# Turning activation blocks by DMA instead of by TensorE: B/C rows, three residual blocks ahead of each MLP, the fourth ahead of the gates

## What is computed

```python
def mamba2_mixer(hn, w_in, conv_w, ...):
    zxbcdt = hn @ w_in
    xbc = jax.nn.silu(causal_depthwise_conv(xbc, conv_w, conv_b))   # xs, bm, cm are parts of xbc
    ...
def sq_relu_mlp(hn, w1, w2):
    return jnp.square(jax.nn.relu(hn @ w1)) @ w2
def per_layer_input(h, p_i, g, w_gate, w_proj):
    gate = jax.nn.sigmoid(rmsnorm(h, g) @ w_gate)
    return h + gate * (p_i @ w_proj)
def reference(...):
    for i in range(DEPTH):
        h = h + mixer(rmsnorm(h, ln_mix[i]))
        h = h + sq_relu_mlp(rmsnorm(h, ln_mlp[i]), mlp_w1[i], mlp_w2[i])
        h = per_layer_input(h, p[i], ple_norm[i], ple_gate_w[i], ple_proj_w[i])
    return h
```

## Time and profile before

| | us |
|---|---|
| median of 3 runs | 2545.94 (2545.83 to 2546.37) |
| the profiled execution | 2546.43 |
| its span, first to last instruction | 2544.7 |
| PE busy | 2537.2 |
| DVE busy | 1646.3 |
| ACT busy | 1339.2 |
| mean busy share of the DMA queue of SP | 68.7% |

### The profile page before, as it was taken

One profiled execution on the slowest core, in us unless ns is written; L12 is line 12 of the kernel. 1 busy time (PEld: TensorE's weight loads), 2 busy tenths in 40 slices (PEclk: granted clock), 3 DMA queues, 4 the chain that ended last, 5 costly groups with the idle time before them and its releaser, 6 DMA issues.

```text
span 2544.7 us, 29493 instructions
## 1 busy us (share of the span) xinstructions
PE 2537.2 (100%) x11668; PEld 2113.4 (83%) x11668; DVE 1646.3 (65%) x1735; ACT 1339.2 (53%) x1674; POOL 100.5 (4%) x208
## 2 busy tenths in 40 slices
PE   9999999999999999999999999999999999999999
PEld 8888888888888888888888888888888888888887
DVE  7678878888755565565557667766655655546564
ACT  6555556656544454443546657655544434434553
POOL 2010000000000000000000002100000000000000
PEclk9999999999999999999999999999999999999999
DMA  8688887887586776776777764446867767767763
GB/s 262 198 246 242 240 244 236 235 231 212 175 229 200 198 217 199 200 219 195 209 213 213 209 188 141 140 154 191 220 192 203 217 193 211 209 194 219 211 207 133
DMA packets 350250, 524.49 MB, mean 206 GB/s; under 512 B 108432, under 2 KB 113800, under 8 KB 350112
## 3 DMA queue, kind: packets, MB, share of 16 engines
q1 hardware_dynamic: 345936, 512.39, 68.7%
q0 software_dynamic: 2656, 8.58, 1.3%
q10 hardware_dynamic: 1520, 1.64, 0.2%
HBM read 486.38 MB, written 2.16 MB: 192 GB/s over the span
## 4 chain that ended last, share of the span: by engine, by line
PE 100%; DMA 0%; DVE 0%; ACT 0%; ACTq 0%; issue 0%
PE acc_a L1936 13%; PE acc_a L1938 13%; PE acc_a L1937 13%; PE acc_b L1936 13%; PE acc_b L1938 13%; PE acc_b L1937 13%; PE mid L1938 5%; PE mid L1936 5%; PE mid L1937 5%; PE tp L1983 1%; PE mid L2116 1%; PE acc_b L2055 1%; PE mid L2319 0%; PE tp L2339 0%; PE tp L2113 0%; DMA h<-in_x 0%
## 5 line engine op out<-in xcount | busy, mean ns | idle before, releaser
L1270 DVE TENSOR_TENSOR w<-raw,w 128x1024 fp32r<-128x1024 f32 (+1 forms) x872 | 1058.6, 1220 | 770.4 <-ACT w L679 767.7
L679 ACT ACTIVATE w<-raw 128x1024 fp32r<-128x1024 f32 (+1 forms) x872 | 916.0, 1055 | 996.2 <-PE acc_b L1938 411.4
L1936 PE MATMUL acc_a<-w,xa 128*128 128x512 f32 x768 | 301.8, 393 | 0.0
L1938 PE MATMUL acc_a<-w,xa 128*128 128x512 f32 x768 | 299.2, 390 | 0.0
L1937 PE MATMUL acc_a<-w,xa 128*128 128x512 f32 x768 | 298.9, 389 | 0.0
L1936 PE MATMUL acc_b<-w,ya_hi 128*128 128x512 f32 x736 | 288.4, 392 | 0.0
L1938 PE MATMUL acc_b<-w,ya_lo 128*128 128x512 f32 x736 | 286.6, 389 | 0.0
L1937 PE MATMUL acc_b<-w,ya_hi 128*128 128x512 f32 x736 | 286.4, 389 | 0.0
L1936 PE MATMUL acc_b<-w,xa 128*128 128x512 f32 (+1 forms) x728 | 282.8, 388 | 0.0
L1938 PE MATMUL acc_b<-w,xa 128*128 128x512 f32 (+1 forms) x728 | 280.1, 385 | 0.0
L1937 PE MATMUL acc_b<-w,xa 128*128 128x512 f32 (+1 forms) x728 | 279.8, 384 | 0.0
(11 more groups left out here) (332 smaller groups left out, 2934.9 us busy)
## 6 DMA issues: line engine op xcount, KB each, us to landing
raw<-in_mlp_w SPq DMA_DIRECT2D x512, 512.0 KB, 4.0
raw<-in_ssm_in_w SPq DMA_DIRECT2D x161, 512.0 KB, 5.7
raw<-in_ssm_out_w SPq DMA_DIRECT2D x64, 512.0 KB, 5.7
raw<-in_ple_gate_w SPq DMA_DIRECT2D x64, 512.0 KB, 4.2
raw<-in_mla_out_w SPq DMA_DIRECT2D x32, 512.0 KB, 3.7
rows<-in_ssm_conv_w SPq DMA_DIRECT2D x32, 256.0 KB, 6.5
scratch<-cumulative POOLq DMA_DIRECT2D x16, 512.0 KB, 7.1
raw<-in_ple_proj_w SPq DMA_DIRECT2D x8, 512.0 KB, 4.4
```

What stands on the lines that cost most here:

```text
L679: act.activation(w_hi[:, g % SPL, :, 0:cols], raw[:, g % RAW, :, 0:cols], ACT.Copy)\
L1270: dve.tensor_tensor(w_lo[:, g % SPL, :, 0:cols], raw[:, g % RAW, :, 0:cols], w_hi[:, g % SPL, :, 0:cols].bitcast(F32), ALU.subtract).then_ ...
L1936: pe.matmul(dst, xh, wh, start=first and k == 0, stop=False)
L1938: mm = pe.matmul(dst, xl, wh, start=False, stop=last and k == 1)
```

## The change

What it does, by places:

- The B and C rows are turned by DMA: `row_words_out` on ACT (2 copies for each block), 2 transposing DMAs on SP, `join_rows` on DVE, in buffers of their own, and the convolution reads `row_joined`. `turn_rows` goes from PE. The convolution's taps stand behind three rests instead of one.
- Of the four blocks ahead of each MLP, block 0 is still turned by PE; blocks 1 to 3 by DMA. The first two up units are interleaved (`UP_FIRST`): 4 chunks read block 0, 4 read block 1, and so on.
- Block 3 ahead of the gates is turned by DMA; the first two gate units are interleaved by `DOWN_FIRST`, so that block 3 is first read in chunk 12.
- `words` and `turned` become two buffers each. Words of block n still wait for the join of block n-2 (`jn`).
- POOL issues its first decay transfer ahead of its wait for the convolved B and C.

In all PE loses 12 turns of 8 transposes, and ACT, SP and DVE get 12 turned blocks more (53 instead of 41).

```diff
+UP_FIRST = [(j, k) for blk in range(4) for j in range(2) for k in (2 * blk, 2 * blk + 1)]
+UP_TURNS = (8, 10, 12), (6, 8, 11)
...
@@ SP
+            def turn_rows():
+                sp.wait_ge(S["rwd"], w.tick("rwd") + 1)
+                for t in range(NT):
+                    sp.dma_start_transpose(row_turned[...], row_words[:, t]...).then_inc(S["rtr"], 16)
...
-                unit(up, c512(0))
+                for m, (j, k) in enumerate(UP_FIRST):
+                    load(u[:, 2 * k:2 * k + 2, c512(512 * j)])
+                    if m in UP_TURNS[layer]:
+                        turn_block()
...
+                for m, (n, k) in enumerate(DOWN_FIRST):
+                    load(g[:, 2 * k:2 * k + 2, c512(512 * n)])
+                    if m in (1, 9):
+                        turn_block()
@@ POOL
-            pool.wait_ge(S["si"], 4)
+                if i == 0:
+                    pool.wait_ge(S["si"], 4)
@@ ACT
                 def job(before=None):
+                    n = w.tick("wd")
+                    words = words_of_two[n % 2]
                     act.wait_ge(S["hadd"], w.now("hadd") + 1)
-                    act.wait_ge(S["jn"], w.tick("wd"))
+                    if n > 1:
+                        act.wait_ge(S["jn"], n - 1)
...
-                unit({2: [act_hi(tiles(xa, 2))], 3: [product(0)]}, halves=4)
-                jobs = {m: [own_before(product(m + 1), 4)] for m in range(3)}
-                jobs[3] = [sums(n, 3), act_hi(tiles(xa, 3))]
+                unit({0: [own_before(product(1), 4)], 1: [own_before(product(2), 4), words_of(3), sums(n, 3)],
+                      2: [own_before(product(3), 4)], 6: [act_hi(tiles(xa, 3))]}, halves=16)
...
-            mlp(0, "BA", {1: [sums(1, 1), act_hi(tiles(xa, 1))], 3: [sums(1, 2), act_hi(tiles(xa, 2))],
-                          5: [sums(1, 3), act_hi(tiles(xa, 3))]})
+            mlp(0, "BA", {0: [words_of(1), sums(1, 1)], 2: [words_of(2), sums(1, 2)], 4: [words_of(3), sums(1, 3)],
+                          5: [act_hi(tiles(xa, 1))], 8: [act_hi(tiles(xa, 2))], 10: [act_hi(tiles(xa, 3))]})
...
-            unit({4: [sums(4, 0), act_hi(tiles(xa, 0))], 6: [sums(4, 1), act_hi(tiles(xa, 1))]}, halves=7)
-            mlp(1, "AB", {1: [sums(4, 2), act_hi(tiles(xa, 2))], 4: [sums(4, 3), act_hi(tiles(xa, 3))]})
+            unit({4: [sums(4, 0), act_hi(tiles(xa, 0))], 5: [words_of(1), sums(4, 1)]}, halves=7)
+            mlp(1, "AB", {0: [words_of(2), sums(4, 2)], 3: [act_hi(tiles(xa, 1)), words_of(3), sums(4, 3)],
+                          5: [act_hi(tiles(xa, 2))], 8: [act_hi(tiles(xa, 3))]})
@@ DVE
-            mlp(0, "BA", {0: [lo(tiles(xa, 0))], 1: [add_out(2), gain(V_MLP + 4), add_out(3)], 2: [lo(tiles(xa, 1))],
-                          3: [gain(V_MLP + 8)], 4: [lo(tiles(xa, 2))],
-                          5: [gain(V_MLP + 12)], 6: [lo(tiles(xa, 3))]})
+            mlp(0, "BA", {0: [lo(tiles(xa, 0))], 1: [add_out(2)], 3: [add_out(3)], 4: [join, in_gain(4)],
+                          6: [lo(tiles(xa, 1))], 7: [join, in_gain(8)], 8: [lo(tiles(xa, 2))],
+                          9: [join, in_gain(12)], 11: [lo(tiles(xa, 3))]})
...
+            mlp(1, "AB", {1: [lambda before: add("B", 3, 0)(before)], 2: [join, in_gain(20)], 3: [lo(tiles(xa, 1))],
+                          4: [join, in_gain(24)], 6: [lo(tiles(xa, 2))], 7: [join, in_gain(28)], 9: [lo(tiles(xa, 3))]})
@@ PE
-            out_piece(OUT_TAIL[2], {3: [turn_h(0, 29)], 6: [turn_h(1, 30)]})
+            out_piece(OUT_TAIL[2], {3: [turn_h(0, 29)]})
...
-                up(0, turns, needs(posted))
+                for j, k in UP_FIRST:
+                    if j == 0 and k % 2 == 0:
+                        pe.wait_ge(S["act"], need[k // 2])
+                    chunk(xa, 2 * k, pairs[j], k == 0, k == 7)
...
-                    if n == 1:
-                        turn_h(3, base + 4)()
-                unit(xa, pp[0], "gs", None, [c + 1, c + 3, c + 4, c + 5])
+                for n, k in DOWN_FIRST:
+                    if n == 0 and k % 2 == 0:
+                        pe.wait_ge(S["act"], need[k // 2])
+                    chunk(xa, 2 * k, pp[n], k == 0, k == 7)
...
-                if n:
-                    turn_h(n - 1, 60 + n)()
+                if n == 1:
+                    turn_h(0, 61)()
```

More of the change, by code:

```diff
@@ L190, in trunk_kernel @@
         at[0] = 0
-        prj, p_sb = part(NT, D), part(NT, PLE)
-        words = part(NT * 512).bitcast(U16).rearrange("p (t s n) -> p t s n", t=NT, s=2)
-        turned = part(4 * TOK).bitcast(U16).rearrange("p (s f n) -> p s f n", s=2, f=4)
+        prj = part(NT, D)
+        p_sb = r_sb[:, 0, :].rearrange("p (t n) -> p t n", t=NT)
+        words_of_two = [part(NT * 512).bitcast(U16).rearrange("p (t s n) -> p t s n", t=NT, s=2) for _ in range(2)]
+        turned_of_two = [part(4 * TOK).bitcast(U16).rearrange("p (s f n) -> p s f n", s=2, f=4) for _ in range(2)]
         joined = part(4, TOK)
@@ L209, in trunk_kernel @@
         ksq = sqf[:, :, 0:512]
-        table = [part(NT, HALF) for _ in range(4)]
+        table = [hq[:, n].rearrange("p (t d) -> p t d", t=NT) for n in range(4)]
         acc_a, acc_b = [ctx.enter_context(nc.psum_tensor(f"acc_{n}", [P, 2, 512], F32)) for n in "ab"]
@@ L253, in trunk_kernel @@
             "wd",
-            "tr",
             "jn",
@@ L280, in trunk_kernel @@
             "xr",
-            "Tc",
+            "rwd",
+            "rtr",
+            "rjn",
             "c0",
@@ L333, in trunk_kernel @@
             "To")}
+        s_turned = [sem(f"turned{n}") for n in range(2)]
         s_lag = [None] + [sem(f"lagged{n}") for n in range(1, CONV_W)]
@@ L480, in gates @@
                     load(v[:, :, c512(512 * n)])
-                for n in range(NB):
-                    jobs = {1: [turn_block]} if n == 0 else {5: [turn_block]} if n > 1 and layer == 0 else {}
-                    unit(ple_gate_w[layer], c512(512 * n), 0, jobs)
+                g = row_tiles(ple_gate_w[layer])
+                for m, (n, k) in enumerate(DOWN_FIRST):
+                    load(g[:, 2 * k:2 * k + 2, c512(512 * n)])
+                    if m in (1, 9):
+                        turn_block()
+                unit(ple_gate_w[layer], c512(2 * 512))
+                unit(ple_gate_w[layer], c512(3 * 512), 0, {3: [turn_block], 6: [turn_block]} if layer == 0 else None)
             mlp(0)
@@ L2173, in mlp @@
                 base = 32 + 32 * layer + 12
-                up(0, turns, needs(posted))
+                w.skip("act", 3)
+                w.skip("tm", 3)
+                w.skip("wd", 3)
+                need = needs(4)
+                pairs = pp[0], "M"
+                for pair in pairs:
+                    hold(pair, "wd")
+                for j, k in UP_FIRST:
+                    if j == 0 and k % 2 == 0:
+                        pe.wait_ge(S["act"], need[k // 2])
+                    chunk(xa, 2 * k, pairs[j], k == 0, k == 7)
                 for q in range(4):
-                    for j in range(1, 4):
+                    for j in range(1 if q else 2, 4):
                         up(j)
@@ L2200, in mlp @@
                     chunk(pt, 0, pair, True, True)
-                    if n == 1:
-                        turn_h(3, base + 4)()
-                unit(xa, pp[0], "gs", None, [c + 1, c + 3, c + 4, c + 5])
-                for n in range(2 + (layer == 0)):
-                    unit(xa, pp[(n + 1) % 2], "gs")
+                w.skip("act")
+                need = c + 1, c + 3, c + 4, c + 5
+                for pair in pp:
+                    hold(pair, "gs")
+                for n, k in DOWN_FIRST:
+                    if n == 0 and k % 2 == 0:
+                        pe.wait_ge(S["act"], need[k // 2])
+                    chunk(xa, 2 * k, pp[n], k == 0, k == 7)
+                for n in range(1 + (layer == 0)):
+                    unit(xa, pp[n], "gs")
                 if layer == 0:
                     w.skip("act", 3)
+                    w.skip("wd", 3)
                 if layer:
```

191 lines of the change are left out of this document (106 added, 85 removed).

## The result

The changed kernel takes **2551.09 us** in the median of 20 runs (2549.89 to 2552.88), the kernel before 2546.43 (20 runs beside them, 2545.67 to 2548.76): a ratio of 1.0017, 95% interval 1.001 to 1.0024. The forecast was 2547.0 with a range of 2537 to 2553. So the time lies in the range, and the best estimate, 0.17% slower, lies inside the 0.2% that were called "same". But it is 4.1 us above the forecast (3.6 if the forecast of +1.1 is set on the before of 2546.43) and all but on the rival "the clock falls behind the 7.2 us wait" (2550.6), and that rival's mechanism is what the trace shows. The profiled execution has 2549.99 us with a span of 2548.3, 3.6 above that of before. One of the 26 executions of the kernel before that stand beside experiments 1 to 4 took 4300.93 us at a mean granted clock of 0.555 and is left out of every comparison.

The account below looks back on a forecast made before the run. PE, busy for 2537.2 of 2544.7 us, was taken to bound the kernel. Terms -10.9 + 0 + 0 + 7.2 + 4.8 = +1.1 us on 2546.43 gave 2547.5, less 0.49 for the median: 2547.0, range 2537 to 2553.

Parts of the forecast that it names:

- the clock falls behind the 7.2 us wait: Rival at the first MLP's start: PE's clock drops to half speed, 3.6 us lost, 2550.6 us; chance 0.22.
- Twelve turns, 10.9 us, starts count and not durations: PE loses 12 turns at 0.91 us each, 10.9 us; rival by durations: 27.4 us saved, 2530.5, chance 0.03.
- B/C rows and gates at nothing: Turning B/C rows and the gates' block 3 by DMA costs PE 0 us; bound of 1 us for B/C.
- First start, 7.2 us of waiting: Start of the first MLP: PE waits 7.2 us in one gap at chunk 4, the first to read block 1.
- Second start, 4.8 us: Start of the second MLP: PE waits in four pieces, 0.75, 0.55, 2.55 and 0.95, sum 4.8 us.
- The sum: Whole kernel: -10.9 + 0 + 0 + 7.2 + 4.8 = +1.1 us on the profiled execution; chance 0.42.
- Late landing: Rival at both MLP starts: DMA-turned block lands too late, up to 2562.4 us; chance 0.15 including other longer chains.
- PE hardly waits: Rival at the MLP starts: all the gain stays, 2535.0 us, or 2539.8 with small waits alone; chance 0.18.

Follow-up runs that it names:

- experiment 4: Changed kernel with the three blocks ahead of each MLP turned by PE again, first up units still interleaved; 2542.37 us.
- experiment 3: Changed kernel with 48 transposes that nobody reads put on PE ahead of chunk 4 of the first MLP; 2550.34 us.
- reordered kernel, both_orders: Kernel of experiment 1: changed kernel with another order on ACT and DVE at both MLP starts; 2535.3 us.
- experiment 2: Changed kernel with the other order on ACT and DVE at the first MLP's start alone; 2540.81 us.
- experiment 1: Changed kernel with another order of the same instructions on ACT and DVE at both MLP starts; 2535.3 us, ratio 0.9954 to the kernel before.
- both_orders_again: Repeat on another occasion of the changed kernel with the other ACT and DVE order at both MLP starts; 2535.83 us.
- second_order: Changed kernel with the other order on ACT and DVE at the second MLP's start alone; 2545.79 us.
- fill24: Changed kernel with 24 transposes that nobody reads put on PE ahead of chunk 4 of the first MLP; 2551.16 us.
- Experiment 7: Kernel fill24: changed kernel with 24 transposes that nobody reads on PE ahead of chunk 4 of the first MLP; 2551.16 us.
- after: The changed kernel itself, first measurement and profile; 2551.09 us in the median, 2549.99 us in the profiled execution.
- after_again: The changed kernel unchanged, measured and profiled a second time; 2550.53 us.
- third_words: Changed kernel with a separate words buffer for block 3, in effect at the first MLP alone; 2549.86 us.
- first_order: Kernel of experiment 2: changed kernel with the other ACT and DVE order at the first MLP's start alone; 2540.81 us.
- first_order_again: Repeat of first_order, the changed kernel with the other ACT and DVE order at the first MLP's start alone; 2540.49 us.
- fill48: Kernel of experiment 3: changed kernel with 48 transposes that nobody reads ahead of chunk 4 of the first MLP; 2550.34 us.

## Why the prediction was right or wrong, point by point

**Twelve turns, 10.9 us, starts count and not durations: right.** Removed per stretch: 3.68 in the B/C rows (from the turns at 18.73 and 18.26 to block 0), 2.71, 0.90, 2.75 and 0.91, in all 10.95. The B/C part takes 4 turns, so 0.92 each. The Trainium skill's figure of 275 ns for one transpose (TensorE: Matmul & The Clock Gate, PE-mode transpose) is a duration that the trace shows as well; as a price it would be 2.4 times too much.

**B/C rows and gates at nothing: right,** by the columns of the table that don't hold a start, and by experiment 4.

**First start, 7.2 us of waiting: right in sum, one step missed.** The forecast was one gap. There are two, 0.56 us of pitch at chunk 0 and 6.56 at chunk 4, together 7.1; with the small delays around them the start lost 7.48 (experiment 3). The small one ends with the addition of block 2, which empties `acc_b` for chunk 0:

```profile
672.47 1.22 DVE L1307 TENSOR_TENSOR w<-raw,w 128x1024 fp32r<-128x1024 f32 x1 [1.72 <-ACT w L711]
673.61 1.28 DVE L1387 TENSOR_TENSOR h<-acc_b,h 128x512 f32<-128x512 f32 x2
```

It stands behind rest 1, and that waited for split 1, which stands behind the words and sums of block 1. In the reordered kernel the addition starts at 672.48, and chunk 0 doesn't wait. The walk had both numbers, the addition at 679.0 and PE at chunk 0 at 678.5, and didn't set them against each other. The gap at chunk 4 ends when DVE is done, whenever PE came there, which is why the sum stayed.

**Second start, 4.8 us: right.** Forecast 0.75, 0.55, 2.55, 0.95. By pitch, where the clock holds (experiment 2): 0.86, 0.41, 2.50, 0.73, which is 4.5; the landmark column, with the small delays between them, gives 688.65 - 683.61 = 5.04.

**The clock: wrong.** This is the step that failed: the sum has no term for the clock, put at nothing because ACT and DVE catch up meanwhile and four chunks lie ready. They do, and it doesn't matter: what lies ready is then worked at half speed. At the first start that cost 690.10 - 688.38 = 1.72 us (other executions 2.12 and 2.84), at the second 689.35 - 688.65 = 0.7 net, since slow matmuls give ACT and DVE time and the fourth wait vanishes. The rival's price of 3.6, "half of the wait", was too simple as a rule: a part of the low level lies inside the wait, where it costs nothing. As a sum it came near, 2.4 at both starts in the profile, but by luck: it had 3.6 at the first start and nothing at the second, and the waits were 0.5 longer than the 12.0 forecast. The forecast's range held the time although this term was missing.

**The sum.** Forecast +1.1 on the profiled execution. Measured: -10.95 + 7.48 + 1.72 + 5.04 + 0.70 = +4.0; the stretch up to the first landmarks was 0.47 shorter in this execution than in that of before, which leaves the +3.5 of the ledger. The medians are 4.7 apart; that their difference is larger than that of the profiles fits the first fall's price, which changes from run to run, but only the profiled executions show it directly.

**Late landing: fell.** A join 7.6 us behind its words doesn't wait. The 10 us that were taken for issue and landing, 4.71 and 5.3 added, were at least 2.4 too many: in the changed kernel the two DMAs of this block are issued one behind the other from 670.28 to 673.45, and each lands 4.0 to 4.5 us behind the start of its own issue, so the second is issued while the first runs. **PE hardly waits: fell,** as a forecast of this order. Its claim that only another order could do it is what experiment 1 shows, and my reason against it, that no slack could hide 18 us of ACT work in front of block 1, was wrong twice. The rows of the changed kernel count 14.2 us between split 0 and the high part of block 1 (words 5.7, sums 3.7, five splits 4.8), and 4.1 of these (words and sums of block 3, one split) needn't stand there: the reordered kernel has 10.1.

## What to carry to other kernels

Work moved from the bounding engine to engines that are idle for a third to a half of the time (DVE 35%, ACT 47%) isn't free by that. Here it was where each moved piece stood behind what the bounding engine wants next, and not where it stood ahead: give every item on ACT and DVE its due time and sort by it. Here a sort that changed no instruction turned +4.7 us into -11. And when a walk predicts a wait of several microseconds on TensorE, charge the clock's fall as well: here 1.7 to 2.8 us behind a wait of 6.4 us, and 0.7 net or nothing behind one of 2.3.

## What the hardware showed that was not expected

**A start that varies.** Block 0's turn ahead of the first MLP begins at 662.5 to 663.0 us in eight profiles without the four B/C turns, and at 664.6 to 665.2 in three (both_orders_again, second_order, fill24), and both_orders_again has the distances of both_orders behind it. The 2 us are lost in the program's first 13 us. Of both_orders and of both_orders_again:

```profile
7.63 0.82 PE L2067 MATMUL acc_b<-ident 128*128 128x128 f32 x6
8.20 3.02 PE L2110 MATMUL acc_b<-w,xa 128*128 128x512 f32 x12
```

```profile
7.84 1.49 PE L2067 MATMUL acc_b<-ident 128*128 128x128 f32 x6
8.98 4.17 PE L2110 MATMUL acc_b<-w,xa 128*128 128x512 f32 x12
```

The next group starts at 11.06 and at 13.00: the same 18 matmuls take 5.2 us in place of 3.4. The windows there say 1.00 in both, so no view shows why. Some 2 us of the differences between whole executions can come from ahead of the first landmarks. Distances between landmarks are free of it, medians aren't.

**The fall of the clock.** Around waits of 6.4, 4.0 and 3.8 us at the first start it fell in five profiles of five; a wait of 1.2 us behind 48 transposes didn't. The Trainium skill (TensorE: Matmul & The Clock Gate, section on the HAM clock gate) says that an idle engine falls to 1.2 GHz and comes back when it is busy; the windows above show both. The section on PE-mode transpose of the same page says further that a transpose doesn't count as busy for that gate in the same way. Taken at its word, filler could not have helped. Experiment 3 speaks against it, if the page means transposes like these, which no view shows: 48 of them kept the clock at 1.00. Experiment 7 points the same way, more weakly, as it is one execution against one: with 24 the clock was still at 1.00 between 690 and 692, where second_order, whose block 0 was turned within 0.1 us of the same time and which has no filler, had 0.74.

**The second start is not settled.** The same waits (0.9, 0.4, 2.5 us by pitch) were followed by a fall in four profiles (after, after_again, third_words, fill24) and by none in three (first_order, first_order_again, fill48). The four have a fall at the first start too, the three don't. The two starts are over 1060 us apart, and no run here tells whether they are linked or whether it is the moment at which the wait begins.
